# Encoder layer with a bidirectional RWKV-7 state: values turned and centred once a pair and loaded as token rows

## The reference, cut to what matters

```python
def step(S, inp):
    r_t, w_t, kh_t, ak_t, v_t, kt_t = inp
    sk = jnp.einsum('bhvk,bhk->bhv', S, kh_t)
    S = S * w_t[:, :, None, :] - sk[..., None] * ak_t[:, :, None, :] + v_t[..., None] * kt_t[:, :, None, :]
    return S, jnp.einsum('bhvk,bhk->bhv', S, r_t)
...
o = _layernorm(o, gn_g.reshape(H, N), gn_b.reshape(H, N), GN_EPS)
```

## Time and profile before

| what | value |
|---|---|
| median of 3 runs | 3368.04 us (3367.3 to 3372.46) |
| the profiled execution, its own time | 3366.02 us |
| its span | 3364.2 us |
| PE busy | 3225.1 us (96%) |
| DVE, ACT busy | 1810.2 us (54%), 1040.5 us (31%) |
| DMA, mean over the span | 98 GB/s |

### The profile page before, as it was taken

One profiled execution on the slowest core, in us unless ns is written; L12 is line 12 of the kernel. 1 busy time (PEld: TensorE's weight loads), 2 busy tenths in 40 slices (PEclk: granted clock), 3 DMA queues, 4 the chain that ended last, 5 costly groups with the idle time before them and its releaser, 6 DMA issues. The chain is left out here.

```text
span 3364.2 us, 59848 instructions
## 1 busy us (share of the span) xinstructions
PE 3225.1 (96%) x25992; PEld 2048.5 (61%) x25992; DVE 1810.2 (54%) x3002; ACT 1040.5 (31%) x1590; POOL 2.5 (0%) x13
## 2 busy tenths in 40 slices
PE   9999999999999899999999999998999999999997
PEld 4564564554555555577778554565666666666665
DVE  1337762677767579055666332155645445645445
ACT  2336652334334123333434451002321111221111
POOL 0000000000000000000000000000000000000000
PEclk9999999999999999999999999998999999999998
DMA  3221101334534423265654224111212212222211
GB/s 137 58 70 32 45 33 48 121 119 149 184 121 133 176 103 135 106 189 164 172 166 120 91 86 153 61 51 54 65 57 76 69 64 68 69 88 75 69 63 63
DMA packets 218532, 328.51 MB, mean 98 GB/s; under 512 B 55456, under 2 KB 176544, under 8 KB 213152
## 3 DMA queue, kind: packets, MB, share of 16 engines
q1 hardware_dynamic: 218272, 324.69, 29.7%
HBM read 221.74 MB, written 96.34 MB: 95 GB/s over the span
## 5 line engine op out<-in xcount | busy, mean ns | idle before, releaser
L624 PE MATMUL ra_ps<-xT,ring 128*128 128x512 f32 (+1 forms) x1152 | 429.8, 526 | 0.0
L1782 PE MATMUL tl_ps<-merged,pool 128*128 128x320 f32 x1440 | 408.5, 436 | 6.4 <-PEq L108 3.9
L1782 PEld LDWEIGHTS tl_ps<-merged,pool 128*128 128x128 f32 x1440 | 275.6, 192 | 124.6 <-issue 13.1
L624 PEld LDWEIGHTS ra_ps<-xT,ring 128*128 128x128 f32 x1152 | 214.3, 190 | 198.9 <-issue 189.3
L1975 DVE TENSOR_TENSOR oR<-tl_ps,oR 128x320 f32<-128x320 f32 x416 | 202.3, 490 | 150.7 <-PE tl_ps L1782 148.4
L1069 PE MATMUL rg_ps<-xT,ring 128*128 128x512 f32 (+1 forms) x720 | 266.0, 525 | 6.0 <-PEq L108 6.0
L1782 PE MATMUL tl_ps<-tl_Th,pool 128*128 128x320 f32 x720 | 204.1, 435 | 6.1 <-issue 6.1
L1069 PEld LDWEIGHTS rg_ps<-xT,ring 128*128 128x128 f32 x720 | 134.8, 191 | 117.2 <-issue 111.7
L1863 ACT ACTIVATE ring<-tl_ps 128x320 f32<-128x320 f32 x96 | 42.0, 437 | 526.6 <-PE tl_ps L1782 526.6
L1782 PE MATMUL tl_ps<-xT,pool 128*128 128x320 f32 x640 | 183.5, 434 | 0.0
L1981 DVE TENSOR_TENSOR merged<-tl_ps,ring 128x320 f32<-128x320 f32 x96 | 47.2, 492 | 252.8 <-PE tl_ps L1782 135.0
(11 more groups left out here) (241 smaller groups left out, 4639.5 us busy)
## 6 DMA issues: line engine op xcount, KB each, us to landing
pool<-ub SPq DMA_DIRECT2D x320, 160.0 KB, 2.8
ub<-ra_ub SPq DMA_DIRECT2D x32, 1280.0 KB, 5.3
pool<-in_w_ff SPq DMA_DIRECT2D x32, 1024.0 KB, 4.8
pool<-in_w_ff SPq DMA_DIRECT2D x64, 512.0 KB, 3.5
ring<-in_w_in SPq DMA_DIRECT2D x39, 512.0 KB, 3.7
xT<-in_xT SPq DMA_DIRECT2D x16, 640.0 KB, 8.2
ub<-ra_v SPq DMA_DIRECT2D x16, 640.0 KB, 6.8
mg_gate<-gates SPq DMA_DIRECT2D x16, 640.0 KB, 4.0
```

The source lines that it names most:

```text
L624: last = pe.matmul(ps[:, bank + j, 0:n], w[c][:, 128 * i:128 * i + 128], xT[:, i, t0:t0 + n], start=(i == 0), stop=(i == KT - 1))
L1782: last = pe.matmul(bank(n, b), lhs(k), rhs(k), start=(fresh and k == 0), stop=(k == d - 1), skip_group_check=True)
```

## The change

In the scaled stage, ten matmuls a pair turn v against a centring matrix of 128x128 (the 64x64 one twice on the diagonal), in three groups of 4, 4 and 2 blocks of 128 tokens into bank 5, among the pieces of the next pair; ACT copies them to `vt`, and SP stores them as token rows of 256 bytes per head to a new array `vt`. The two stores of v go. Units of `ub` have four blocks of 64 columns instead of five and are stored contiguously. In the state stage the value matmuls and ACT's two evictions a step go; SP loads the value rows of step g + 2 (4 loads of 64 rows of 1 KB) straight into `X`, which has three buffers now and the order (head, unit, column); the units come in four loads of two units, 256 KB each. The identity for the scores moves to the fifth block. The output is the same.

```diff
@@ scaled_stage @@
-                sp.dma_start(hbm["ub"][p, d][:, HC * hf:HC * hf + HC, CH:5 * CH], ub[n % 3][:, :, :]).then_inc(ub_sent[n % 3], 16)
+                sp.dma_start(hbm["ub"][p, d][:, HC * hf:HC * hf + HC, :], ub[n % 3][:, :, :]).then_inc(ub_sent[n % 3], 16)
+
+            def send_values(p):
+                for i, (t0, n) in enumerate(TURNS):
+                    sp.wait_ge(vt_done, 3 * p + i + 1)
+                    for h in range(2):
+                        sp.dma_start(hbm["vt"][p // 4, 128 * t0:128 * t0 + 128 * n, h, CH * (p % 4):CH * (p % 4) + CH].rearrange(
+                            "(t p) n -> p t n", p=128), vt[:, t0:t0 + n, CH * h:CH * h + CH]).then_inc(v_sent, 16)
...
+                if p:
+                    send_values(p - 1)
                 if p == PAIRS:
                     gate_out(0)
...
-                if p < PAIRS:
-                    sp.wait_ge(mix_s[2], p + 1)
-                    sp.wait_ge(mix_p[2], p + 1)
-                    for d in range(2):
-                        sp.dma_start(hbm["ub"][p, d][:, :, 0:CH], v[:, :].rearrange("p (c n) -> p c n", n=CH)).then_inc(v_sent, 16)
...
+            def turn(p, i):
+
+                t0, n = TURNS[i]
+                if i == 0:
+                    pe.wait_ge(mix_s[2], p + 1)
+                    pe.wait_ge(mix_p[2], p + 1)
+                else:
+                    pe.wait_ge(vt_done, 3 * p + i)
+                for t in range(n):
+                    last = pe.matmul(ps[:, 5, 128 * t:128 * t + 128], v[:, 128 * (t0 + t):128 * (t0 + t) + 128], centre,
+                                     start=True, stop=True)
+                last.then_inc(vt_ready, 1)
...
                     lower(p - 1, 0, 3)
+                    turn(p - 1, 0)
                 after(pe, mix_p[2], p)
                 span(0, 0, 2)
                 low_piece(p, 0, 2)
+                if p:
+                    turn(p - 1, 1)
...
                     lower(p - 1, 1, 6)
+                    turn(p - 1, 2)
                 span(1, 3, 1)
                 low_piece(p, 1, 0)
+                after(pe, vt_done, 3 * p)
                 span(1, 3, 2)
...
                     lower(PAIRS - 1, 1, 6)
+                turn(PAIRS - 1, j)
+                if j == 2:
+                    pe.wait_ge(vt_done, 3 * PAIRS)
...
+            def values_out(p, i):
+                t0, n = TURNS[i]
+                act.wait_ge(vt_ready, 3 * p + i + 1)
+                if i == 0:
+                    after(act, v_sent, 96 * p)
+                act.activation(vt[:, t0:t0 + n, :].rearrange("p t n -> p (t n)"), ps[:, 5, 0:128 * n], ACT.Copy).then_inc(vt_done, 1)
...
                     lower_out(p - 1, 0)
+                    values_out(p - 1, 0)
                 scale_own(p, 0, k, 1)
                 sigmoids(p, 0, 2)
                 if p:
+                    values_out(p - 1, 1)
                     lower_out(p - 1, 1)
+                    values_out(p - 1, 2)
@@ state_stage @@
+            def load_values(g, d, h):
+                t0 = CH * chunk_of(g, d)
+                sp.dma_start(X[g % 3][64 - 64 * h:128 - 64 * h, h, 4 * d:4 * d + 4, :].rearrange("p u n -> p (u n)"),
+                             hbm["vt"][g // NCH, t0:t0 + CH, h, :]).then_inc(vt_ready[g % 3], 16)
...
                     sp.wait_ge(b_ready, g + 1)
-                    load_unit(sp, hbm, ub[g % 3], g + 3, 0, ub_ready[g % 3])
-                if g + 3 < NSTEP:
+                    load_two(sp, hbm, ub[g % 3], g + 3, 0, ub_ready[g % 3])
+                if g + 2 < NSTEP:
                     sp.wait_ge(sc_ready, 4 * g + 7)
-                    load_unit(sp, hbm, ub[g % 3], g + 3, 1, ub_ready[g % 3])
+                    after(sp, o_ready, g)
+                    load_values(g + 2, 0, 0)
+                if g + 2 < NSTEP:
+                    load_values(g + 2, 0, 1)
...
-                    if u == U - 1:
-                        last.then_inc(bd_ready, 1)
-                    if g + 1 < NSTEP:
-                        values(g + 1, u)
+                last.then_inc(bd_ready, 1)
                 if g + 1 < NSTEP:
                     scores(g + 1, 1)
-                pe.wait_ge(v_done, 2 * g + 2)
+                pe.wait_ge(vt_ready[g % 3], 64 * (g // 3) + 64)
...
                 if g + 1 < NSTEP:
                     transposes(g + 1, 0)
-                    act.wait_ge(v_ready, g + 2)
-                    if g:
-                        act.wait_ge(o_ready, g)
-                    evict(g + 1)
                     transposes(g + 1, 1)
@@ the load of two units @@
+def load_two(sp, hbm, ub, g, i, ready):
+
+    d, q = i // 2, 4 * (g // NCH) + 2 * (i % 2)
+    sp.dma_start(ub[:, 2 * i:2 * i + 2, 0:4 * CH],
+                 hbm["ub"][q:q + 2, d, :, chunk_of(g, d), :].rearrange("q p n -> p q n")).then_inc(ready, 16)
```

More of the change, by code:

```diff
@@ L36 @@
 C_CEN = C_ID64 + 64
-NCONST = C_CEN + 64
+NCONST = C_CEN + 128
 (P_MP, P_MN, P_W0, P_A0, P_KK, P_KA, P_RK, P_GG, P_GB) = (0, 3, 6, 8, 10, 11, 12, 13, 14)
@@ L789, in _ @@
                 sigmoids(p, 1, 2)
-                after(act, v_sent, 32 * p)
+                after(act, vt_ready, 3 * p)
                 after(act, bonus_done, p)
@@ L807, in _ @@
                 if c:
+                    for i in range(2):
+                        values_out(PAIRS - 1, i)
                     lower_out(PAIRS - 1, 1)
+                    values_out(PAIRS - 1, 2)
                 act.wait_ge(gate_ready, c + 1)
@@ L927, in pv_at @@
     return 160 * d + NCH * p + c
-UCOLS = 8 * 6 * CH
-POOL_COLS = 3 * UCOLS
+UCOLS = 8 * 5 * CH
+POOL_COLS = 8 * D + T // 2
 def units_of(pool):
-    return [pool[:, UCOLS * i:UCOLS * i + UCOLS].rearrange("p (u n) -> p u n", n=6 * CH) for i in range(3)]
+    return [pool[:, UCOLS * i:UCOLS * i + UCOLS].rearrange("p (u n) -> p u n", n=5 * CH) for i in range(3)]
 def weights_of_tail(pool):
@@ L1031, in _ @@
                 if b in (6, 7):
-                    for u in range(8):
-                        load_unit(sp, hbm, ub[b - 6], b - 6, u, ub_ready[b - 6])
+                    for i in range(4):
+                        load_two(sp, hbm, ub[b - 6], b - 6, i, ub_ready[b - 6])
                 sp.wait_ge(gate_done, b + 1)
@@ L1163, in state_stage @@
         KTt = [st.sb(f"KT{i}", 128, U, 2, CH) for i in range(2)]
-        X = [st.sb(f"X{i}", 128, U, 2, CH) for i in range(2)]
+        X = [st.sb(f"X{i}", 128, 2, U, CH) for i in range(2)]
+        X.append(pool[:, 3 * UCOLS:3 * UCOLS + 2 * U * CH].rearrange("p (h u n) -> p h u n", h=2, n=CH))
         NF = st.sb("NF", 128, U, CH)
@@ L1211, in _ @@
                 if m == 0:
-                    for u in range(U):
-                        load_unit(sp, hbm, ub[2], 2, u, ub_ready[2])
+                    for g in range(2):
+                        for i in range(4):
+                            load_values(g, i // 2, i % 2)
+                    for i in range(4):
+                        load_two(sp, hbm, ub[2], 2, i, ub_ready[2])
             for g in range(NSTEP):
@@ L1262, in scores @@
                         rows = slice(64 * h, 64 * h + 64)
-                        last = pe.matmul(ps[:, 4 + 2 * (q % 2) + h, 192 * j:192 * j + 192], x[rows, 2 * q + j, CH:3 * CH],
-                                         x[rows, 2 * q + j, 3 * CH:6 * CH], start=True, stop=True)
+                        last = pe.matmul(ps[:, 4 + 2 * (q % 2) + h, 192 * j:192 * j + 192], x[rows, 2 * q + j, 0:2 * CH],
+                                         x[rows, 2 * q + j, 2 * CH:5 * CH], start=True, stop=True)
                 last.then_inc(sc_ready, 1)
-            def values(g, u):
-                for h in range(2):
-                    last = pe.matmul(ps[other(h), UB, CH * u:CH * u + CH], ub[g % 3][half(h), u, 0:CH], centre[half(h)],
-                                     start=True, stop=True)
-                if u == U - 1:
-                    last.then_inc(v_ready, 1)
             def heads(out, bank, lhsT, rhs, start, skip=True):
@@ L1290, in _ @@
                 scores(0, q)
-            for u in range(U):
-                values(0, u)
             for g in range(NSTEP):
-                x, sc, v = ub[g % 3], SC[g % 2], X[g % 2]
+                x, sc, v = ub[g % 3], SC[g % 2], X[g % 3]
                 if g + 1 < NSTEP:
@@ L1330, in _ @@
                     for h in range(2):
-                        pe.matmul(ps[half(h), OB, CH * u:CH * u + CH], S[half(h), u, :], x[half(h), u, 4 * CH:5 * CH],
+                        pe.matmul(ps[half(h), OB, CH * u:CH * u + CH], S[half(h), u, :], x[half(h), u, 3 * CH:4 * CH],
                                   start=u == 0, stop=True, skip_group_check=True)
                     for h in range(2):
-                        last = pe.matmul(ps[half(h), BB, CH * u:CH * u + CH], sc[other(h), u, h, 0:CH], v[other(h), u, h, :],
+                        last = pe.matmul(ps[half(h), BB, CH * u:CH * u + CH], sc[other(h), u, h, 0:CH], v[other(h), h, u, :],
```

(9 more changed lines are left out.)

60 lines of the change are left out of this document (26 added, 34 removed).

## The result

The changed kernel takes 3371.76 us (median of 22 runs), the kernel before, run beside it on the same chip, 3366.69 us (22 runs): ratio 1.0016, 95% interval 1.0009 to 1.0022. So it is slower by 5 us, where a gain of 8.5 us was forecast; 3371.76 lies inside the range given, 3347 to 3380. The profiled execution of after has a span of 3367.1 us against 3364.2. Further down, times of other kernels are compared by their ratio to before on their own chip (before had medians of 3360.5 to 3370.6 us there), and stage by stage from one profiled execution each. The five kernels that reach the scaled stage 2 to 3 us earlier than the rest (at 521 to 522 us) owe this to the attention stage, which no edit touches; a difference of 3 us in one span says nothing.

A forecast was written before the change was run, and what follows sets the result against it. It took TensorE to bound the kernel, by its work in the scaled stage and by missing instructions in the state stage. Scaled +22.4 and state -30.9 gave -8.5 us from the median 3368.04: 3359.5 us, range 3347 to 3380.

The forecast's parts named there:

- TensorE runs out of instructions: State stage: stalls without a semaphore come from late instruction pages; an average step loses 1.01 us, 38 us in all.
- The values lie in the idle quarters: State stage: value matmuls run in the other array quarters under L1317; removing them shortens that phase 0.02 us a step.
- I leave a quarter of the loss: State stage: removing the value matmuls' instructions gains 28 of the 38 us lost in stalls; a quarter stays.
- a deficit against a lead of 66: State stage: some 66 instructions stand ready ahead; the dense run's shortage falls from 128 to 65, which they just cover.
- Cost nothing: State stage: SP's eight loads a step, four now 256 KB, add no time, being issued over half a step before their readers.
- Turns, 17.4 us: Scaled stage: 80 added 128x128 f32 matmuls at 0.2175 us each, all on the path; upper end 30 us.
- The last wait: Scaled stage's end: after the last turn TensorE waits for ACT's last eviction, behind a 0.7 us copy: 0.9 us.
- A page late in a lower product: Scaled stage: added instructions may make a page late in one of 16 lower products: 1 us taken, 0 to 3.
- The queue at the end: Scaled stage's end: stores and loads issued together make the last store land later, delaying the gate stage: 3.1 us, bounds 0 and 6.
- signs written down: Predicted signs: scaled stage 17 to 20 us longer, L1317 unchanged, steps 9.7 to 9.8 us, waits under 10, some 87 pages.
- Rival B: State stage: half the loss stays because the OB, n and NF run stays dense; 3368 to 3373 us, chance 0.23.
- Rival C: State stage: stalls are not instruction supply, or page position decides, not density; gain only 2.9 us, about 3387, chance 0.14.

The follow-up runs named there:

- e1: Changed kernel with 16 f32 matmuls a step put back in the array's idle quarters, their result read by nobody: 3409.93 us, ratio 1.0124 to the kernel before.
- e9: e8 with the second score product of each step moved into the middle of the OB product: ratio 0.9992 to the kernel before.
- e5: Changed kernel with the units in eight loads of 128 KB a step in place of four of 256 KB: ratio 0.9997 to the kernel before.
- e8: Changed kernel with e5, e2, e6 and a new order at the scaled stage's end (early gate store, early last turn) together: 3358.75 us, ratio 0.9963 to before.
- e4: Kernel before with four loads of two units (320 KB) a step in place of eight of 160 KB: ratio 1.0028 to the kernel before.
- e2: Changed kernel with the six value stores of a pair issued by SP behind the pair's weight loads: ratio 1.0001 to the kernel before.
- e6: Changed kernel with each lower product of the pairs cut in two, half a span of the projection between: 3366.98 us, ratio 0.9988 to the kernel before.
- e12: e8 with the second score product of each step halved, two matmuls ahead of OB and two in its middle: ratio 0.9988 to the kernel before.
- e11: Kernel before with its eight 160 KB loads a step issued two at a time, at the changed kernel's four places: ratio 1.0006 to the kernel before.

## Why the prediction was wrong

The step that failed is the weighing of the instruction supply, in three terms that were read from averages: the stage that grew got 1 us for late pages in the lower products, where some 8 came; the state stage was to lose three quarters of its stops and lost about half; and the larger loads were put at nothing. The first weight load of each turn group, 2.6 us, was missing as well. The 61 instructions per us of the prediction are what TensorE used on average (254 in 4.21 us), not what the queue can bring: a page is fetched once per border, and is usable 3.2 to 4 us after the border before. So it is the time between two borders that counts, not a deficit against a rate.

**TensorE runs out of instructions: right.** e1 and e9 show it from both sides. The rule that was weighed (Trainium skill, Runtime: NRT & Kernel Launch, section Instruction fetch mechanics) is borne out in its block of 256 instructions and in the time at which the next one is asked for; "mostly hidden" does not hold in the dense code of the steps: 39 us of stops in 38 of them.

**The values lie in the idle quarters: right.** Without them the phase takes 1.08 us (L1354, 1524.09 to 1525.17), with them 1.09.

**"I leave a quarter of the loss": too small.** At borders 39.2 us became 18.1, almost half; with loads of 128 KB (e5, e8) 11.7 and 14.3 were left, so a good part of this miss is the next item. The count of a deficit against a lead of 66 took the dense run as one block. It is the 256 instructions ahead of each border that count, and 15 of the 18 at 301 to 415 still stop. State stage -24.9 us, forecast -31.

**The loads "Cost nothing": wrong.** The bound "a loss of 9, if the same bytes in 256 KB loads delay each of some 90 pages by 0.1 us" named the mechanism; e4 measured 12.8 us on the kernel before, some 4.5 of them by the clock, and e5 3 to 4 on the changed one. I left it out of the value taken because transfers land long before their readers. What came late was instructions, which the row on landings does not cover.

**Turns, 17.4 us: nearly right.** 80 x 0.2225 = 17.8. Missing was the first weight load of each of 24 groups, 0.11 us: 2.6. The last wait, 0.9 forecast, was 0.7. From matmul start to matmul start the turns hold 21.5 us, with that wait and 0.5 us of half clock.

**"A page late in a lower product", 1 us (0 to 3): the largest miss.** Measured 6.3 us in the products, 0.3 behind one, and about 1.5 (an estimate) in the 3 us at half clock that follow the long stop. I had the mechanism and not its arithmetic: no border of before fell into the window, and the ten matmuls added per pair (40 instructions) move every border. The bound of 3 us was taken from one late page of up to 2 us; the long stop was 3.0 with the value stores out of the way (e2) and 4.2 with them.

**The queue at the end, 3.1 us: right** (2.7).

Together: scaled stage +27.0 for +19.3, end +2.7 for +3.1, state -24.9 for -31, gate +1.6 for 0, and -3.5 behind, where nothing was changed. The terms named for the scaled stage add up to 29; the other 2 us came back in the spans, whose own time fell by 0.6 us although 0.3 and most of the half clock lie in it. That they start behind a turn now, and not behind a lower product, is the likely reason, not tested. Of the signs written down, the L1317 phase, the pages (86), the turn matmul and the idle time of 8.7 us came true; the scaled stage (17 to 20), the average step (9.90 for 9.7 to 9.8) and the waits (12.6 for under 10) did not. Rival B had this size ("3368 to 3373", half the loss stays), and of its two reasons the dense second run was the true one. Rival C's half sentence, "the page's position and not the density decides", is true of the lower products, where position decides whether there is a stop at all.

## What to carry to other kernels

Look for "issue" waits inside one loop and number the instructions: if they share a remainder, the cost of an instruction is not its array time. Then any added or removed matmul moves all borders behind it, and a few us either way follow that belong to no edit; judge such an edit by its stage without those stops, and keep dense runs of small matmuls shorter than a page, with long ones between, where the cut costs nothing (e6 gained 5.6 us by it; e9 and e12 lost in their steps what the stops gave). Transfers that no engine waits for can still cost time through later pages.

## What the runs showed that I had not expected

- Sixteen idle-quarter matmuls a step, read by nobody, cost 42.5 us in 38 steps of the profiled execution (36 by the ratios), about one us a step, with no change in any undisturbed phase. Some 8 of the 42.5 are the half clock.
- A DMA of 320 KB in place of two of 160 KB at the same moment costs 12.7 us in 38 steps (e4 against e11), in which the pages come 0.11 us later; the two issued together cost nothing (399.5 against 399.4).
- After 4.2 us without a matmul the granted clock is 0.50 (1.2 GHz) for 3 us, and a turn's matmul takes twice its time. In e1, e4 and e11 the same came six, three and three times in the 38 steps, each time behind a stop of 1.2 to 1.9 us, at a price of some 1.5 us. After itself has a stop of 1.4 us in its steps without it, so what decides is open.
- Each beginning of a score product shows a gap of 0.15 us and each end one of 0.25 us, so evening out the code has a price of its own. A score product placed between OB and n was not tried.
